# An encoder layer on one core: its MLP written as seven block products in place of eight, with the block sums on GpSimd and VectorE

## The reference

```python
def squared_relu_mlp(hn, w_up, w_down):
    return jnp.square(jax.nn.relu(hn @ w_up)) @ w_down
...
        h = h + squared_relu_mlp(rms_norm(h, mlp_norm[l]), mlp_w_up[l], mlp_w_down[l])
    return rms_norm(h, final_norm)
```

## Time and profile before

| | |
|---|---|
| median of 3 runs | 2134.67 us (2133.46 to 2136.58) |
| the profiled execution | 2135.16 us, of which its span in the trace is 2133.3 us |
| PE busy | 1945.4 us, 91% of the span |
| DVE, ACT, POOL busy | 851.4, 440.7, 457.9 us (40%, 21%, 21%) |
| chain that ended last | PE 84%, of it 47% at L691; DVE 9% |

### The profile page before, as it was taken

The page is one execution under the profiler, slowest core; times in us unless marked ns, Lnnn a source line. Parts: engine busy times, 40 slices in busy tenths (PEclk is TensorE's granted clock), DMA queues, the critical chain, the costliest instruction groups (busy, mean ns, idle before and its releaser), DMA issues.

```text
span 2133.3 us, 25685 instructions
## 1 busy us (share of the span) xinstructions
PE 1945.4 (91%) x10028; PEld 1520.7 (71%) x10028; DVE 851.4 (40%) x1123; ACT 440.7 (21%) x788; POOL 457.9 (21%) x283
## 2 busy tenths in 40 slices
PE   5999999988888888858889978999999999999996
PEld 4767676646676677637787745888888888888885
DVE  6522323244646564444351054335215304413533
ACT  3222222242313232231031031121001001101110
POOL 2210211020201010012103220333333333333330
PEclk9999999977989999968989989999999999999998
DMA  5100010003020202022132100111111111111111
GB/s 205 40 20 18 20 38 18 4 10 75 15 70 21 61 21 49 1 86 83 39 116 73 38 10 10 49 49 41 48 49 49 49 49 49 49 49 49 39 49 79
DMA packets 76358, 100.89 MB, mean 47 GB/s; under 512 B 28928, under 2 KB 56064, under 8 KB 76032
## 3 DMA queue, kind: packets, MB, share of 16 engines
q1 hardware_dynamic: 76288, 99.90, 15.0%
HBM read 86.76 MB, written 13.12 MB: 47 GB/s over the span
## 4 chain that ended last, share of the span: by engine, by line
PE 84%; DVE 9%; ACT 3%; issue 2%; DMA 1%; POOL 0%; SPq 0%; DVEq 0%; ACTq 0%; POOLq 0%
PE PS L691 47%; PE PS L739 6%; PE PS L834 3%; PE PS L863 3%; PE PS L891 2%; PE PS L848 2%; PE PS L1262 2%; PE PS L1078 1%; PE PS L888 1%; PE PS L1199 1%; PE PS L1042 1%; PE PS L940 1%; PE PS L1026 1%; PE PS L800 1%; PE PS L1052 1%
## 5 line engine op out<-in xcount | busy, mean ns | idle before, releaser
L691 PE MATMUL PS<-xn,wsp 128*128 128x512 f32 x2880 | 661.6, 392 | 9.4 <-DVE xn L1680 6.2
L691 PEld LDWEIGHTS PS<-xn,wsp 128*128 128x128 f32 x2880 | 544.3, 189 | 125.7 <-issue 7.4
L691 PE MATMUL PS<-hid,wsp 128*128 128x512 f32 x1536 | 349.4, 389 | 0.0
L691 PEld LDWEIGHTS PS<-hid,wsp 128*128 128x128 f32 x1536 | 288.2, 188 | 59.7
L577 POOL CAST wsp<-wraw 128x1024 fp32r<-128x1024 f32 x104 | 110.5, 1063 | 1011.0 <-PE PS L691 696.1
L579 POOL TENSOR_TENSOR wsp<-wraw,wsp 128x1024 fp32r<-128x1024 f32 x104 | 262.6, 2525 | 8.3
L739 PE MATMUL PS<-xn,wsp 128*128 128x512 f32 x576 | 146.7, 401 | 4.2 <-DVE proj L1730 4.2
L2221 DVE TENSOR_TENSOR tmp<-tmp,ssum 128x1024 f32<-128x1024 f32 x32 | 81.8, 2556 | 127.1 <-ACT tmp L1635 127.0
L739 PEld LDWEIGHTS PS<-xn,wsp 128*128 128x128 f32 x576 | 104.7, 189 | 36.0 <-issue 15.9
L1635 ACT ACTIVATE tmp<-PS 128x1024 f32<-128x1024 f32 x32 | 32.9, 1027 | 392.0 <-PE PS L691 384.6
L2235 DVE TENSOR_TENSOR H<-PS,H 128x1024 f32 x24 | 29.4, 1224 | 210.5 <-PE PS L691 210.5
(11 more groups left out here) (274 smaller groups left out, 2339.0 us busy)
## 6 DMA issues: line engine op xcount, KB each, us to landing
wraw<-in_weights_dram SPq DMA_DIRECT2D x120, 512.0 KB, 3.5
H<-in_x_dram SPq DMA_DIRECT2D x16, 512.0 KB, 6.7
H<-x_dram SPq DMA_DIRECT2D x32, 128.0 KB, 2.5
H<-xt_dram SPq DMA_DIRECT2D x32, 128.0 KB, 2.6
out_dram<-proj SPq DMA_DIRECT2D x8, 512.0 KB, 3.6
a_dram<-H SPq DMA_DIRECT2D x12, 256.0 KB, 2.3
o_dram<-o_stage SPq DMA_DIRECT2D x3, 512.0 KB, 2.7
ssum<-in_head_weights_dram SPq DMA_DIRECT2D x4, 320.0 KB, 3.9
```

Source lines behind the costliest of these rows:

```text
L691: last = nc.tensor.matmul(PS[:, 2 * k + half, :], wsp[:, k, kt, a, :], src[:, kt, b, HALF * half:HALF * half + HALF], start=(kt == 0 and ( ...
```

## The change

Each of the eight 1024 x 1024 products is cut into 2 x 2 blocks of 512 and made from seven block products in place of eight (Strassen's scheme in Winograd's form). The code calls a 1024 x 1024 product a gemm, n = 0 to 7 (even n: up, odd n: down), its block products parts, in the order P1, P2, P6, P7, P4, P5, P3, and each part has four slots, one for each output tile of 128 x 512. A slot is 4 contraction tiles x 3 half products = 12 matmuls into one bank of PSUM; seven banks go round. There are 8 x 7 x 4 = 224 slots.

In place of a unit's two POOL instructions, a slot has a cast by ScalarE (`w_high`) and a subtraction by GpSimd (L803); GpSimd also makes the four block sums of the weights, 16 of them in a gemm (L787). The input of a slot is no longer split once: ScalarE and VectorE split one input tile of 128 x 512 per slot (`x_high`, L2496 `x_low`), and VectorE makes four block sums of the input, 16 tiles, in each odd gemm and in gemm 0 (L2453). The output blocks are sums of products; VectorE adds them up in `evict` (L2514): one or two additions that read PSUM per slot, in an odd gemm one more of two SBUF tiles in the slots of P7, P4 and P5, in an even gemm a ReLU with the factor (L2564) in those of P2, P4, P5 and P3. ScalarE squares. The final norm goes in two halves of 512 positions, the first beside the last products. The engines' loops are unrolled; at step g each engine does what stands in the diff. The raw weights come in quarters and halves of the old tiles: `quarter(n, j, part)` loads 256 KB of `w11` or `w12`, or 512 KB of `w21` with `w22`; those of gemm 0 for P1 early, the other 3 MB after the last unit of `U_O`. Where a buffer comes free by another engine's work, a count is waited for: an input tile of part q is split into a ring of 8 tiles, so not before the last slot of part q-2 is done, and a weight tile into a ring of 6.

```diff
+            sp.wait_ge(C_DVE.sem, C_DVE.at("l3", 1))
+            for j in range(ROWS):
+                quarter(0, j, 11)
+            sp.wait_ge(acc_ready, U_MLP - 1 + 3)
+            for part in (12, 2):
+                for j in range(ROWS):
+                    quarter(0, j, part)
...
-            split_weights(U_O, UNITS - U_O)
+            split_weights(U_O, U_MLP - U_O)
...
+            for g in range(SLOT_END):
+                n, part, j = part_of(g)
+                if g == slot(0, P2, 0):
+                    for k in range(ROWS):
+                        sum_s1(0, k)
+                w = w_split_of(g)
+                pool.wait_ge(mw_head, g + 1)
+                nc.gpsimd.tensor_tensor(w[:, 1, :], w_source(g), w[:, 0, :].bitcast(F32), ALU.subtract).then_inc(mw_rest, 1)
...
+                elif n and part == P1:
+                    pool.wait_ge(mw_rest, g + 1)
+                    w_at(f"s1_{n}_{j}")
+                    w_add(f"s2_{n}_{j}", rw_11[j], rw_21[j], rw_11[j], ALU.subtract)
+                if part == P2:
...
+                    w_add(f"s4_{n}_{j}", rw_12[j], rw_12[j], rw_11[j], ALU.subtract)
+                if part == P6:
...
+                    w_add(f"s3_{n}_{j}", rw_11[j], rw_22[j], rw_11[j], ALU.subtract)
+                if part == P3 and n < GEMMS - 1:
+                    sum_s1(n + 1, j)
...
+            def product(g):
...
+                pe.wait_ge(mw_rest, g + 1)
+                bank_ready(g)
+                for k in range(ROWS):
+                    d = slot(n, part, k)
+                    x = x_split_of(d)
+                    if j == 0:
+                        pe.wait_ge(mx_rest, d + 1)
+                    for a, b in ((0, 0), (0, 1), (1, 0)):
+                        last = nc.tensor.matmul(PS[:, g % PS_BANKS, :], w[:, a, win(k)], x[:, b, :],
+                                                start=(k == 0 and (a, b) == (0, 0)), stop=(k == ROWS - 1 and a == 1))
+                last.then_inc(part_done, 1)
...
+            for g in range(SLOT_END):
+                product(g)
+                if g == slot(0, P1, 1):
+                    norm_sum(2, PS_BANKS)
+                if g == slot(0, P1, 3):
+                    norm_spread(2, PS_BANKS - 1)
+                if g == slot(GEMMS - 1, P5, 2):
+                    final_sum(0)
+                if g == slot(GEMMS - 1, P3, 1):
+                    final_spread(0)
+            final_sum(1)
+            final_spread(1)
...
+            def x_high(d):
...
+                if d >= X_RING:
+                    act.wait_ge(part_done, d // ROWS * ROWS - ROWS)
...
             for kt in range(KT):
                 act.wait_ge(h_added, KT + kt + 1)
...
                 act.wait_ge(sq_added, 2 * KT + kt - 1)
                 square(kt % 2, H[:, kt, :])
...
+                if kt >= ROWS:
+                    x_high(kt - ROWS)
+                if kt >= 6:
+                    w_high(kt - 6)
...
+            for g in range(SLOT_END + 2):
+                if g + 4 < SLOT_END:
+                    w_high(g + 4)
+                if 1 <= g <= SLOT_END:
+                    keep(g - 1)
+                if g >= 2:
+                    square_out(g - 2)
...
+                if g + 5 < SLOT_END:
+                    x_high(g + 5)
...
+            def x_low(d):
...
+                dve.wait_ge(mx_head, d + 1)
+                nc.vector.tensor_tensor(x[:, 1, :], x_source(d), x[:, 0, :].bitcast(F32), ALU.subtract).then_inc(mx_rest, 1)
...
+                dve.wait_ge(part_done, g + 1)
+                if n % 2:
...
+                    if part == P7:
...
+                        add("e", t, src, u)
...
+                        add("va", h21, h21, t)
+                    if part == P4:
...
+                        add("e", h21, src, h21)
...
+                        add("vb", h22, h22, t)
+                    if part == P5:
...
+                        add("u", u, src, u)
...
+                        add("e", h22, src, h22)
...
+                        add("vc", h12, h12, u)
...
+            for g in range(SLOT_END + 1):
+                if g + 5 < SLOT_END:
+                    x_sum(g + 5)
+                if g >= 1:
+                    evict(g - 1)
+                if g >= 3:
+                    final_add(g - 3)
...
+                if g + 4 < SLOT_END:
+                    x_low(g + 4)
```

More of the change, by code:

```diff
@@ L1278, in _ @@
             gemm(U_O, 8, xn, ca_ready)
[L1280 to L1302, removed]
+            def bank_ready(g):
+                if g < PS_BANKS:
+                    if g < 4:
+                        pe.wait_ge(acc_free, U_O + 6 + g // 2 + 3)
+                    if g == PS_BANKS - 1:
+                        pe.wait_ge(factor_made, 1)
+                    return
+                n, part, j = part_of(g - PS_BANKS)
+                if part == P1:
+                    pe.wait_ge(part_kept, ROWS * n + j + 1)
+                if part != P1 or n % 2:
+                    pe.wait_ge(EV.sem, EV.at(f"e{part}_{n}_{j}", -1))
@@ L1643, in _ @@
[L1643 to L1657, removed]
@@ L2239, in hiddens @@
-            def hiddens(c, i0):
-                with dve.Fori(i0, 4) as i:
-                    for k in range(2):
-                        hidden(c, i, k)
-            norm(2)
-            for k in range(2):
-                dve.wait_ge(relu_ready, k + 1)
-                nc.vector.sem_inc(acc_free, 1)
-            dve.wait_ge(nb_ready, 3)
-            nc.vector.tensor_copy(ssum[:, :], two(4)).then_inc(factor_made, 1)
-            dve.wait_ge(factor_made, 1)
-            for k in range(2):
-                hidden(0, 0, k, True)
@@ new lines, in _ @@
+            x_sum(4)
+            last = GEMMS - 1
+            for g in range(SLOT_END + 1):
[5 more added lines that the diff above has]
+                    final_add(g - 3)
+                if g == 2:
+                    norm(2, PS_BANKS)
+                if g == 4:
+                    dve.wait_ge(nb_ready, 3)
+                    nc.vector.tensor_copy(ssum[:, :], two(PS_BANKS - 1)).then_inc(factor_made, 1)
+                if g + 4 < SLOT_END:
+                    x_low(g + 4)
+                if g == slot(last, P5, 3):
+                    final_var(0)
+                if g == slot(last, P3, 0):
+                    final_inverse(0)
+                if g >= slot(last, P3, 2):
+                    for kt in range(2):
+                        final_scale(0, 2 * (g - slot(last, P3, 2)) + kt)
```

447 lines of the change are left out of this document (369 added, 78 removed).

## The result

The changed kernel takes **2145.13 us** (median of 9 runs, 2141.47 to 2150.57) against 2134.67 for the kernel before, measured beside it. The ratio is 1.0049, with a 95% interval of 1.0030 to 1.0068: 0.5% slower. The forecast was 2111, faster. The profiled execution took 2146.97, its span is 2145.2, so 1.8 lie outside it.

The account below looks back on a forecast made before the run. PE's matmul count was taken to bound the kernel while other engines keep up: 1407.8 + 609.4 + 5.3 + 52 + 12 + 7 + 16 = 2109.5, with 1.9 outside the span 2111 us forecast; range 2064 to 2165.

Parts of the forecast that it names:

- MLP start: Where U_O's last unit ends and the MLP's matmuls begin, taken as 1407.8 us.
- No penalty then: MLP matmuls: 12 in a row into one bank still take 0.2267 each, 609.4 us for 2688, 87.0 less.
- Norm groups, stalls, start and clock: PE's other MLP time: norm groups 5.3, waits for late VectorE 52, start 12, clock 7 us.
- End: From the last matmul to the span's end: 16 us in place of 25.4, final norm's first half beside the last slots.
- 0.75 on the mean: Odd P7: a GpSimd operation costs VectorE 0.5 beside a PSUM reader, 1.0 otherwise; slot 3.3 us against PE's 2.72.
- two operations per slot in even P5: VectorE's four slots of even P5 meet two GpSimd operations each, giving an excess of 2.7 us.
- Clock: MLP: after VectorE's runs of lateness the granted clock falls, 1.7 us at every second of eight runs, 7 us (0 to 20).
- Start: Gemm 0: late input tile 4 us, GpSimd's first sums and operations ahead of P2 8; 12 in all (6 to 20).
- The shared port decides: Rival, MLP: VectorE loses GpSimd's whole hold even beside an evict; stalls up to 156, time 2215 us; chance 0.3 for slower.
- GpSimd as PE's pacer: Rival, MLP: GpSimd's 44 operations a gemm pace PE, 27 us in place of 52, time 2086; chance 0.1.
- hidden block sums: Rival, MLP: block sums stay hidden, GpSimd at 1.05, stalls 12 and no clock loss, 2064 us; chance 0.2.
- signs of being wrong: MLP: L803 taking 1.05, PE waiting longest for weights rather than inputs, or low halves waiting for ScalarE.

Follow-up runs that it names:

- e_sums: Changed kernel with only GpSimd's block sums of weights replaced by fills of one column (output not the reference's): 2086.65 us, 0.979 to the kernel before.
- e_both: Changed kernel with odd-gemm additions read from PSUM, and even gemms without the norm's factor, ReLU on ScalarE: 2110.09 us, 0.9889 to the kernel before.
- e_port: Changed kernel with GpSimd's two-operand MLP work replaced by constant fills (output not the reference's): 2063.16 us, 0.966 to the kernel before.
- e_alt: Changed kernel with VectorE's low half placed between the two PSUM readers in P5 of each gemm: 2137.60 us, 1.0008 to the kernel before.
- e_probe2: Changed kernel plus patterns of VectorE's two-SBUF and PSUM-reading operations beside GpSimd's subtraction; with GpSimd free, alternating took 3.35 us, pairs 4.56, each 2.4 alone.
- e_odd: Changed kernel; odd gemms add P7 and P5 straight from PSUM and gather P1 + P6 over the odd gemms: 2131.64 us, 0.9984 to the kernel before.
- e_even: Changed kernel; H multiplied once by the mean square, even gemms' ReLU moved to ScalarE without the factor: 2124.06 us, 0.9951 to the kernel before.
- e_best2: e_best with low halves between PSUM readers in every slot with more than one: 2091.36 us, 0.9796 to the kernel before.
- e_best: e_both with gathered P1 + P6 added in gemm 6, gemm 7 adding them from PSUM, half of H's factor from PSUM: 2101.51 us, 0.9839 to the kernel before.

## Why the prediction was wrong

The span came out at 2145.2 where the sum gave 2109.5. Term by term:

- **MLP start**, 1407.8: the first matmul stands at 1411.0, 3.2 later. That is less than runs differ: 1401.8 in e_sums, 1417.4 in e_both.
- **PE**, 609.4: a matmul that follows with no wait (a pitch of at most 0.245) takes 0.2302 on the mean, 8.7 more in all. "No penalty then" was wrong by 1.5%. e_port has 0.2299, so the port is not the cause; the paragraph on PE's pitch below says where it lies.
- **Norm groups, stalls, start and clock**, 5.3 + 52 + 12 + 7 = 76.3: pitches above 0.245 make up 98.1 beyond 0.2267 each, 21.8 more: 73.0 in 39 pitches of over 0.5 us, most of them waits, and 25.1 in 160 slower matmuls.
- **End**, 16: from the last matmul, 2127.3, it is 17.9, 1.9 more.

Together 35.6 of the 35.7. The third term is the largest, but alone it would have brought 2133, level with the kernel before; the longer pitch and the two small terms made it slower. In e_port the third term is 12.1, so 86.0 of it is what GpSimd's operations cost, where I had 52 + 8 + 7 = 67 for that.

**The step that failed** is the period of VectorE's slots, "0.75 on the mean" per GpSimd operation in odd P7 and two operations per slot in even P5. Prices were right: G 1.30 where nothing held it (1.28 taken), S 0.60 to 0.69, 1.07 lost in a pair (1.04 was the bound), PSUM readers not held. What failed is where GpSimd's operations fall. Odd P7 of the last gemm, VectorE and then GpSimd:

```profile
2081.74 0.68 DVE L2496 TENSOR_TENSOR tmp_r<-sa,tmp_r 128x512 fp32r<-128x512 f32 x1
2082.34 1.78 DVE L2453 TENSOR_TENSOR sa<-sa 128x512 f32<-128x512 f32 x1
...
2085.36 0.68 DVE L2496 TENSOR_TENSOR tmp_r<-sa,tmp_r 128x512 fp32r<-128x512 f32 x1
...
2081.80 1.77 POOL L803 TENSOR_TENSOR wsp<-sa,wsp 128x512 fp32r<-128x512 f32 x1 [1.85 <-ACT wsp L1828]
2085.43 1.77 POOL L803 TENSOR_TENSOR wraw_r<-sa,wraw_r 128x512 fp32r<-128x512 f32 x1 [1.85 <-ACT wraw_r L1828]
```

Every slot looks alike: GpSimd is released just after the low half has begun (by 0.06 and 0.07 us), waits for it, and then holds the block sum behind it for its whole length. An average over chance positions is no price here; the position repeats. The slot takes 3.62 where I had 3.3. In even P5 GpSimd was already at P3's work (the rows of P5 above show L787, which has no operation in P5) and put ten operations into VectorE's four slots, not eight: up to 4.7 a slot in place of 3.4. e_alt's slot and e_probe2 bear out the rule behind it for a GpSimd that has work waiting: it takes its turn after an S, and what stands next on VectorE decides the loss. Odd P5 (3.5 for 3.4) was right; even P3 took 3.7 to 4.0 on the mean for 3.6. A pair of an odd and an even gemm stalls 20.3 us on the mean of three; less the 2.1 of e_port, which is the longer pitch, it is 18.2, where I had 12.9 and 1.75 for the clock. These three pairs make about 11 of the 19 us between 67 and 86. The fourth, the last gemm with P7 to P3 of the first, makes about 9: it costs 23.5 more than in e_port, and P5 of the last gemm alone stalls 8.7, beside the final norm.

**PE's pitch.** The ring of eight split inputs has six tiles in `memr` and two in `tmp_r`, so every second part reads `tmp_r`. PE's rows in e_port with no wait between them:

```profile
1562.38 6.96 PE L1458 MATMUL PS<-memr,wsp 128*128 128x512 f32 x30
1569.17 1.57 PE L1458 MATMUL PS<-tmp_r,wsp 128*128 128x512 f32 x6
1570.58 1.55 PE L1458 MATMUL PS<-memr,wsp 128*128 128x512 f32 x6
1571.98 1.56 PE L1458 MATMUL PS<-tmp_r,wsp 128*128 128x512 f32 x6
```

From start to start 30 matmuls on `memr` follow at 0.226, the six on `tmp_r` at 0.235 and the next six on `memr` at 0.233. So it is throughout e_port: a part that reads `tmp_r` follows at 0.2330 from its first such matmul on, the next eight matmuls are slow as well, and the last three slots of a part on `memr` alone follow at 0.2267, the pitch of the kernel before. Twelve matmuls in a row into one bank thus cost nothing, as the prediction read from its rows; the penalty goes with where the inputs lie. Why a tile in `tmp_r` costs this stays open, and no run moved it.

**Clock.** Twelve stretches after a wait show matmuls at about 0.43, 93 of them with 18.5 us in excess, where I counted four stretches at 1.7. One of them, in two windows:

```profile
1676.40:1682.00 5.60, 5.60 (x14) 4.40 (x15) 5.53 (x7) 1.77 (x4) 4.80 (x4) 0.51 0.00 0
1682.00:1695.00 13.00, 13.00 (x58) 10.62 (x57) 12.90 (x13) 7.33 (x14) 9.43 (x7) 1.00 0.01 1
```

PE had waited 3.62 for a low half; the granted clock is then 0.51, about 1.2 GHz of the two levels, for 5.6 us, and 1.00 again after. Most of these stretches are followed by another wait for VectorE, which had no idle time in between (after eight of the twelve); there the slow matmuls probably took the place of waiting, as the prediction said of the inside of a run. How much of the 25.1 us adds to the end was not separated.

**Start.** P1 of the first gemm stalls 10.5, and 9.8 in e_port: not the port's doing, but the norm's groups (3.5) and the late inputs, 6 to 7 for the 4 I took. P2 and P6, where GpSimd makes the first sums, stall 7.7, and 0.4 in e_port: the port's, and the 8 that I took for them was about right.

**The rivals.** "The shared port decides" came nearest, at its near end. What it feared, that the waiting operation is issued right after a low half, is what the rows of odd P7 show; that an evict then hides nothing is not, since beside the two PSUM readers of even P5 an operation of GpSimd stayed free. It named 75 us of stalls, beside 7 for the clock, as the point where the gain is gone. Of some 23 us that the sum had left of the gain the port took 19 (86 where I had 67), and the longer pitch more than the rest. GpSimd as PE's pacer is out (4.9 us of waits for weights), hidden block sums too. Two of the signs of being wrong that the prediction named stayed away: the shortest L803 took 1.26, and PE waited longest for inputs, 55 us. They tested the prices, not where the operations fall.

## What to carry to other kernels

When two engines exclude each other, price each meeting at its full length unless the order of instructions guarantees that something unaffected stands beside it; a loop repeats one position, it does not draw one at random. Count the other engine's operations in the window in which they run, not in the slot they belong to: here GpSimd, with its lead, put ten into four slots of even P5. Three remedies paid here, each by itself: to change what an operation reads, PSUM in place of a second SBUF tile (e_odd, 13.5 us), to take two-SBUF operations off VectorE, a part of them over to ScalarE (e_even, 21), and to put a PSUM reader behind an SBUF operation (e_alt, 7.5; e_best2, 10 less than e_best).

## What the runs showed of the hardware

- GpSimd and VectorE take strict turns when both always have work with two SBUF inputs waiting: 1.67 us a pair of 512-wide operations, for 1.22 and 0.60 alone.
- With GpSimd running freely the loss per operation of it goes with VectorE's order: 1.07 in S S S, 0.87 in S E S S, 0.72 in E E S S, 0.47 in E S E S.
- GpSimd's fill of 512 columns (526 ns in e_port) left VectorE's two-input operations at 686 on the mean where they overlap and 685 where they don't: it is GpSimd's work on operands that excludes them.
- Matmuls of the same shape follow at 0.227 in the kernel before and, in e_port, from the second slot on in parts whose inputs lie in `memr` alone; where two of four input tiles lie in `tmp_r` they follow at 0.233. Why stays open.
